# A residual block with 32 streamed experts: which queue issues the lower half of each down matrix

## What is computed

```python
def moe_ffn(h, w_router, b_router, w_gate_up, b_gate_up, w_down, b_down):
    ...
    logits = (xt @ w_router + b_router).astype(jnp.float32)
    top_v, top_i = lax.top_k(logits, TOP_K)          # 4 of 32
    gates = jax.nn.softmax(top_v, axis=-1).astype(h.dtype)
    ...
    def expert_block(args):
        xblk, e = args
        gu = xblk @ w_gate_up[e] + b_gate_up[e]
        x_glu = jnp.minimum(gu[:, :D_EXPERT], SWIGLU_LIMIT)
        x_lin = jnp.clip(gu[:, D_EXPERT:], -SWIGLU_LIMIT, SWIGLU_LIMIT)
        act = x_glu * jax.nn.sigmoid(SWIGLU_ALPHA * x_glu) * (x_lin + 1)
        return act @ w_down[e] + b_down[e]
```

## Time and profile before

| | |
|---|---|
| median of 3 runs | 1178.1 us |
| profiled execution | 1178.92 us |
| its span in the trace | 1176.7 us |
| TensorE busy | 1036.8 us, 88% |
| weights and other data moved | 464.91 MB, mean 395 GB/s |
| on SyncE's queue q1 | 399.55 MB |
| on ScalarE's queue q10 | 64.01 MB |
| granted TensorE clock, mean | 0.948 |

### The profile page before, as it was taken

The page is one execution under the profiler, slowest core; times in us unless marked ns, Lnnn a source line. Parts: engine busy times, 40 slices in busy tenths (PEclk is TensorE's granted clock), DMA queues, the critical chain, the costliest instruction groups (busy, mean ns, idle before and its releaser), DMA issues.

```text
span 1176.7 us, 21858 instructions
## 1 busy us (share of the span) xinstructions
PE 1036.8 (88%) x8299; PEld 502.3 (43%) x8301; DVE 294.9 (25%) x813; ACT 179.9 (15%) x453; POOL 31.3 (3%) x54
## 2 busy tenths in 40 slices
PE   4999999977788999899989998999899889696986
PEld 3847887433342333334333433343334333332333
DVE  4637664241111122111211221122112211111112
ACT  3213340221101111101110111011111111010012
POOL 1001002110000000000000000000000000000000
PEclk9999999978888999999999999999999989898888
DMA  9899925989999999989999999999999999999995
GB/s 350 316 383 383 356 103 226 424 352 424 424 425 424 420 425 426 422 364 410 426 425 426 422 427 426 425 425 426 426 425 426 426 425 425 427 424 425 426 427 235
DMA packets 61484, 464.91 MB, mean 395 GB/s; under 512 B 5900, under 2 KB 10060, under 8 KB 28568
## 3 DMA queue, kind: packets, MB, share of 16 engines
q1 hardware_dynamic: 52096, 399.55, 82.4%
q10 hardware_dynamic: 9032, 64.01, 13.1%
q0 software_dynamic: 336, 1.07, 0.3%
HBM read 462.50 MB, written 2.11 MB: 395 GB/s over the span
## 4 chain that ended last, share of the span: by engine, by line
PE 63%; DMA 25%; DVE 3%; issue 3%; ACT 2%; SPq 2%; ACTq 2%; POOL 0%; DVEq 0%
PE pp L1541 23%; DMA bgu<-in_b_gate_up_dram 13%; PE pp L1572 11%; DMA arena<-in_w_down_dram 11%; PE pp L1327 5%; PE pp L1505 4%; PE pp L1249 4%; PE pp L1340 2%; PE pp L1259 2%; PE po L1402 2%; PE pp L1514 2%; PE po L1486 2%; PE pp L1520 1%; ACT work L712 1%; DMA arena<-in_w_ada_dram 1%
## 5 line engine op out<-in xcount | busy, mean ns | idle before, releaser
L1541 PE MATMUL pp<-arena,work 128*32 128x256 f32 (+1 forms) x3840 | 397.1, 470 | 40.9 <-ACT work L712 40.9
L1541 PEld LDWEIGHTS pp<-arena,work 128*32 128x32 f32 (+1 forms) x3840 | 170.0, 124 | 252.4 <-issue 151.6
L1572 PE MATMUL pp<-arena,work 128*32 128x256 f32 (+1 forms) x1920 | 192.0, 436 | 20.9 <-DMA arena<-in_w_down_dram 13.6
L1093 DVE TENSOR_SCALAR work<-pp 128x128 f32<-128x128 f32 (+1 forms) x74 | 25.0, 338 | 449.8 <-PE pp L1541 449.8
L1572 PEld LDWEIGHTS pp<-arena,work 128*32 128x32 f32 (+1 forms) x1920 | 76.7, 116 | 118.3 <-issue 80.4
L1505 PE MATMUL pp<-h_sb,work 128*32 128x256 f32 (+1 forms) x480 | 68.8, 493 | 39.8 <-DMA bgu<-in_b_gate_up_dram 21.3
L715 ACT ACTIVATE work<-work 128x128 f32<-128x128 f32 (+1 forms) x74 | 25.9, 350 | 426.0 <-DVE work L1093 426.0
L1486 PE MATMUL po<-work 64*128 64x512 f32 x304 | 75.5, 615 | 1.2 <-ACT work L731 1.2
L1087 DVE COPY work<-pp 128x256 f32<-128x256 f32 (+1 forms) x37 | 19.5, 526 | 203.7 <-PE pp L1505 203.7
L1505 PEld LDWEIGHTS pp<-h_sb,work 128*32 128x32 f32 (+1 forms) x480 | 22.4, 125 | 81.5 <-issue 47.8
L1327 PE MATMUL pp<-arena 128*128 128x256 f32 x256 | 57.1, 382 | 0.0
(11 more groups left out here) (224 smaller groups left out, 605.2 us busy)
## 6 DMA issues: line engine op xcount, KB each, us to landing
arena<-in_w_gate_up_dram SPq DMA_DIRECT2D x128, 2048.0 KB, 31.5
arena<-in_w_down_dram SPq DMA_DIRECT2D x32, 2048.0 KB, 34.5
arena<-in_w_down_dram ACTq DMA_DIRECT2D x60, 1024.0 KB, 12.4
arena<-in_w_ada_dram SPq DMA_DIRECT2D x11, 2048.0 KB, 14.4
arena<-in_w_in_dram SPq DMA_DIRECT2D x4, 2048.0 KB, 19.4
arena<-in_w_gate_dram SPq DMA_DIRECT2D x4, 2048.0 KB, 13.9
arena<-in_w_out_dram SPq DMA_DIRECT2D x2, 2048.0 KB, 10.4
arena<-in_w_down_dram SPq DMA_DIRECT2D x4, 1024.0 KB, 16.0
```

What stands on the lines that cost most here:

```text
L1541: mm = t_.matmul(pp[j * m:(j + 1) * m, UP[hh], 0:w].rearrange("p (s f) -> p s f", s=2), hgT[:, at:at + m], gu_w[slot][:, k, :, r * PAIR:(r ...
L1572: mm = t_.matmul(pp[j * m:(j + 1) * m, UP[0], 0:w], actT[:, at:at + m], wd[:, j * w:(j + 1) * w], start=(n == 0), stop=(n == KD - 1))
```

## The change

Issuing the lower half of the down matrix moves from SyncE to ScalarE. ScalarE's loop now handles two places per turn (for the two slots), reads two entries of the order table instead of one, and behind the two upper pages of the next place issues the lower half of the place after it. It does so at `s_y`. SyncE's loop loses the wait on `s_dhi_free` and that load; `s_dhi_free` is still raised and nobody waits for it. The first two lower halves (places 0 and 1) and the last upper half stay with SyncE.

```diff
+        def load_dlo(eng, slot, e):
+            eng.dma_start(dlo_w[slot].rearrange("p (g r) d -> p g (r d)", r=2),
+                         dn_v[e, :, 0:2, :]).then_inc(s_dlo[slot], 16)
...
                     sp.wait_ge(s_gu, total * 2)
                     load_gu(slot, e, 3)
-                    sp.wait_ge(s_dhi_free, total)
-                    load_dlo(slot, e)
                     count_blocks(i * 2 + (1 + slot))
...
-            with act.Fori(1, NEXP - 1) as n:
-                e = act.value_load(expert_i[0:1, bass.ds(n, 1)], min_val=0, max_val=NEXP - 1)
-                act.wait_ge(s_y, item)
-                for r in range(2):
-                    load_dhi(act, e, r)
-                place(n)
+            with act.Fori(0, NEXP // 2 - 1) as i:
+                for slot in range(2):
+                    e = act.value_load(expert_i[0:1, bass.ds(i * 2 + (1 + slot), 1)], min_val=0, max_val=NEXP - 1)
+                    behind = act.value_load(expert_i[0:1, bass.ds(i * 2 + (2 + slot), 1)], min_val=0, max_val=NEXP - 1)
+                    act.wait_ge(s_y, item)
+                    for r in range(2):
+                        load_dhi(act, e, r)
+                    load_dlo(act, slot, behind)
+                    place(act.snap(i * 2 + (1 + slot), min_val=0, max_val=NEXP - 1))
```

More of the change, by code:

```diff
@@ L408, in _ @@
                              src).then_inc(s_page[n % RING], 16)
-            def load_dlo(slot, e):
-                sp.dma_start(dlo_w[slot].rearrange("p (g r) d -> p g (r d)", r=2),
-                             dn_v[e, :, 0:2, :]).then_inc(s_dlo[slot], 16)
             load_bgu(0, 0)
@@ L424, in _ @@
             sp.wait_ge(s_merged, KD)
-            load_dlo(0, 0)
+            load_dlo(sp, 0, 0)
             sp.wait_ge(s_wo0, 1)
@@ L434, in _ @@
             sp.wait_ge(s_hm, 2 * TT)
-            load_dlo(1, 1)
+            load_dlo(sp, 1, 1)
             sp.wait_ge(s_h2, 2 * TT)
```

## The result

The changed kernel takes 1230.6 us (median of 1226.44, 1230.12, 1232.55 and 1231.09). The kernel before, run beside it on the same chip, takes 1178.0. The ratio is 1.0436, with a 95% interval of 1.0410 to 1.0461: **4.4% slower**. The profiled execution is the quickest of the four, 1226.44 us with a span of 1224.2 us, against a span of 1176.7 before. So the traces explain 47.5 us, and the medians differ by 52.6.

What follows compares the result with a forecast made beforehand. The prediction took the expert stage to be bound by its weight stream at 425 GB/s, DMA engines full; terms of +14, +27, +9, +1 and -4 gave +47 us on the 1178.1 median: 1225 us, range 1197 to 1241.

Steps and rivals of the forecast that it cites:

- Run against run, a third of the bytes: Both queues busy: they alternate run by run, so ScalarE's 8 KB against 16 KB gets a third of 425, 142 GB/s.
- The sum: Whole expert stage: +14 to place 10's issue, +27 three patterns, +9 places 22-25, +1 places 26-30, -4 place 31: +47 us.
- Places 1 to 4: Narrow places in a row: upper halves land every 29.6 us, the fourth at 375.2; place 5 starts about 377, +13 us.
- +14 at the issue of place 10: Places 1 to 9 together: +13 from places 1 to 4, net +1 from places 5 to 9, +14 at 542.59 us.
- The pattern of four, 127.0: Narrow, wide, narrow, wide-and-narrow places: 20.0, 30.5, 28.3 and 48.2 us, together 127.0 against 117.9; +9.1 each, three times.
- The lateness itself: ScalarE's extra issue and register load before its copy: 1.1 us in a narrow place, 0.9 in a wide one.
- The waits of the down product: In narrow places (12, 16, 20 and on) the wait for the down matrix grows from a few us to near 10.
- Places 22 to 25: Narrow, wide, narrow, wide: 109.7 us against 101.0 before, +9 us.
- Holes every 127 us: Slices of the weight stream under 400 GB/s recur near the ends of first blocks of places 5, 13, 17, 21.
- Half share: Rival: ScalarE's queue gets half of 425 GB/s for a lower half, no upper half is late: 1186 us, chance 0.13.
- Nothing moves: Rival: same bytes and engines, late upper halves covered by a stream that is behind anyway: 1178 us, chance 0.04.
- faster: Rival: gate/up pages come 4.9 us sooner on SyncE's queue, the hole at 524 closes: 1172.6 us, chance 0.03.

Runs made afterwards that it cites:

- experiment 1: The changed kernel with every gate/up page loaded in two parts, 8 KB runs instead of 16 KB: 1199.5 us, ratio 1.0180.
- experiment 3: The changed kernel with gate/up in 8 KB runs and both down halves in 4 KB runs: 1264.1 us, ratio 1.0725.
- experiment 5: The changed kernel with ScalarE's register loads of the next place moved ahead of its wait for `s_y`: 1220.9 us, ratio 1.0367.
- experiment 11: The changed kernel with gate/up in 8 KB runs and ScalarE's register loads moved ahead of its wait for `s_y`: 1201.0 us, ratio 1.0165.
- experiment 2: The kernel before with gate/up pages in 8 KB runs: 1184.5 us, ratio 1.0047.
- experiment 4: The kernel before with one more register load and one more 2 KB transfer on ScalarE per place: 1214.7 us, ratio 1.0308.

## Why the prediction was right, point by point

It named 1225 us, 1197 to 1241, and measured were 1230.6 (1226.4 in the profiled execution, on whose trace the sum of 47 was made). Where its steps stand:

- **Run against run, a third of the bytes: right.** 195 against 194 counts and 34% of the bytes; experiments 1 and 3 move the share by the length of runs alone, as the law says.
- **The sum: right, and in part by luck.** Said were 14 + 27 + 9 + 1 - 4 = 47 us. By the same steps the trace has 12.9 + 31.2 + 9.1 - 0.6 - 5.0 = 47.5: the three patterns cost 4 us more than said, and each of the other steps but one gives some of it back. Within the patterns, too, errors meet, as told below. And the medians differ by 52.6 us, which is 5 more than the trace that the sum was made for.
- **Places 1 to 4: right.** The fourth upper half lands at 373.4 us (375.2 said), place 5 starts at 375.3 (377).
- **+14 at the issue of place 10: right.** 555.47 against 542.59 us, +12.9.
- **The pattern of four, 127.0: right as a sum, and wrong within.** It takes 127.0, 129.2 and 128.8 us. But the first one's four intervals are 22.9, 31.2, 26.0 and 46.9 us, where 20.0, 30.5, 28.3 and 48.2 were said. The first term, the narrow place that finds ScalarE's queue empty, is under by 3 us in each pattern: 22.9, 23.8 and 22.8 us. It has two roads to the same length. In places 10 and 18 the gate/up product takes 10.3 and 10.2 us; in place 14 it takes 7.5, and TensorE then waits for the upper half. ScalarE and the product in place 10, the product in place 14, and TensorE at the last quarter of the down product of place 14:

```profile
555.47 0.85 ACTq L343 DMA_DIRECT2D arena<-in_w_down_dram  x2
...
558.51 0.37 ACT L710 COPY work<-pp 128x256 f32<-128x256 f32 x1 [3.42 <-issue]
...
558.94:569.25 10.31, 10.31 (x130) 4.93 (x130) 0.38 (x2) 0.06 (x1) 0.00 (x0) 0.71 1.00 424
685.98:693.47 7.49, 7.49 (x130) 4.21 (x130) 0.40 (x2) 0.07 (x1) 0.00 (x0) 1.00 0.99 420
...
702.34 1.93 PE L1573 MATMUL pp<-arena,work 128*32 128x256 f32 x16 [2.65 <-DMA arena<-in_w_down_dram]
```

In place 10 the copy starts 3.04 us after the first issue where it was 2.48, and the product runs at a granted clock of 0.71; the prediction let it keep its old length (9.06 us there). In place 14 the clock is 1.00, but the upper half lands 19.8 us after the first issue where 17.0 was taken (the prediction had seen 19.1 too, and took the lower one), the last quarter takes 1.93 us where it was 1.07, and the next issue comes 4.0 us after the landing and not 2.55. The lateness itself, taken as 1.1 us, is 0.7 in narrow blocks (4.55 to 5.22 us from the gather to the product) and 1.0 in a wide one (4.75 to 5.72). A longer first place lets ScalarE's queue drain further: 9.0 to 10.1 us of work are left behind it where 11.8 were said, and 7.2 to 9.2 behind the wide place (10.9). So the later upper halves wait less, and the third and the fourth interval of this pattern are shorter than said. The sum stays near 127 because the queue sets it: experiment 5 takes the lateness out and still reads 127.
- **The waits of the down product: too high.** "Near 10" was said; they are 3.3 to 4.0 us in places 12, 16 and 20 and 4.7 to 6.7 in places 24, 26, 28 and 30, because TensorE, slower itself, comes to the upper half later. With the lateness gone (experiment 5) they are 9.7.
- **Places 22 to 25: right.** 110.1 us, 109.7 said. Places 26 to 30 take 144.2 (145.4 said), the last one gives back 5.0 (4 said).
- **Holes every 127 us near the ends of the first blocks of places 5, 13, 17, 21: right**, and the one of place 9, which was there before, stays (now 7.6 us).
- **The rivals.** *Half share*, 1186 us, is refuted by the counts; experiment 1 made it come true, and it costs 1199.5 and not 1186. Its own sum lacked 1% of the rate (421 against 425 GB/s, which comes with making the runs even and not with the share), and, as argued in experiment 11, the order of need. *Nothing moves*, 1178 us, and *faster*, 1172.6, fell. The Trainium skill, in the section Issuing engines are not separate DMA queues of DMA: Bandwidth & Descriptors, says that all issuers' transfers interleave on the same engines and a second one saves issue time only. The trace agrees on the first half: both queues' runs interleave one to one, and the full rate is 425 GB/s before and after. On the second the page speaks of what can be saved and not of what can be lost: with ScalarE's lateness taken out on both sides, the choice of queue cost 44.5 us here (1220.9 against 1176.4), by order and share.

**What stays open.** How the 52 us divide is not a sum of parts. Raising the share takes 31 away (experiment 1); of the 21 that remain, 6 are the price of the runs (experiment 2) and 15 are put down to the order of need, which is read from the waits and from the end of experiment 11 and was not removed by an experiment of its own. Nor does it account for all: in the traces experiment 1 is 12 us behind experiment 2, and 9 of these are there by the end of place 9 (550.5 against 541.1 us), where its waits for bias rows add up to only 3.3. The lateness is worth 10 when the share is a third (experiment 5) and nothing when it is a half (experiments 1 and 11 are equal), though by itself it costs 37 in the kernel before when it is somewhat larger (experiment 4). Why the same idle time before a gate/up product goes with a clock of 0.71 in one block and 1.00 in another is not known. Nor was it tried to send the lower half from ScalarE with longer runs than gate/up has. And experiment 3's 1264 us have no account beyond the six issues.

## What to carry to other kernels

The two DMA queues here shared the engines by the length of their runs (195 runs to 194, 2.80 to 1.46 MB), not by what is urgent: before moving a load to the less busy queue, work out that queue's share and ask whether its longest batch fits the shortest interval. Keep loads in one queue in the order in which they are needed; a bulk load that is needed last, put ahead of or beside one with a short deadline, costs either the deadline (at a third of the bytes, experiment 5) or, as experiment 11 is read, the head of the next place (at half). And count every instruction that stands between a semaphore and a copy that TensorE waits for; here the first 0.6 us of it cost 4 us over 30 places and the next 0.6 us 33.

## What the runs showed of the hardware that was not expected

- **Short idle times that come back in every place cost clock, not only themselves, and not by their length alone.** From place 6 on, with 2.6 to 3.4 us of idle before each, the narrow gate/up products of experiment 4 that open a place ran at a granted clock of 0.71 to 0.74 in 9.9 to 10.3 us, and its wide ones with 1.7 to 1.9 us before them at 0.89 to 0.90 in 15.5 to 15.7 us. With 2.1 us before them the kernel before had 1.00, 0.81 and 0.71 in 7.55, 9.05 and 10.28 us. With 0.5 to 0.7 us (the patterns of experiment 5) all ran at 1.00.
- **8 KB runs move 421 GB/s and 16 KB runs 425** with all 16 engines full (700 to 800 us in both): 6 us of this kernel's time.
- **Counts stay equal for each pair of run lengths**: 195 to 194 at 16 KB against 8, 291 to 287 at 8 against 8, 201 to 194 at 8 against 4.
